# Turning normalised blocks by DMA instead of TensorE, and one more MLP quarter as seven products, in an eight-core decoder step

## What is computed

```python
# layer 0: token mixers A (causal pooling) and B (HGRN2 recurrence, 6 heads)
h = rmsnorm(x, norm_mix[0])
mixed = even_layer(h, ...)            # in-projection, pooling, HGRN2, out-projection
x = x + mixed
x = x + square(relu(rmsnorm(x, norm_mlp[0]) @ ff_w1[0])) @ ff_w2[0]     # d_ff = 4096
# layer 1: short gated convolution
x = x + odd_layer(rmsnorm(x, norm_mix[1]), ...)
x = x + square(relu(rmsnorm(x, norm_mlp[1]) @ ff_w1[1])) @ ff_w2[1]
y = rmsnorm(x, norm_final)
# rmsnorm(x, g) = x * rsqrt(mean(x*x) + eps) * g, over the 1024 channels of a token
```

## Time and profile before

| what | value |
|---|---|
| median of 3 runs | 1490.19 us (1487.7 to 1490.36) |
| the profiled execution, slowest core | 1491.38 us |
| its span, first to last instruction | 1489.6 us |
| spans of the eight cores | 1471.7 to 1489.6 us |
| mean granted TensorE clock of the cores | 0.984 to 0.991 |
| busy share of the span | PE 94%, DVE 72%, ACT 57%, POOL 15% |

### The profile page before, as it was taken

One profiled execution on the slowest core, in us unless ns is written; L12 is line 12 of the kernel. 1 busy time (PEld: TensorE's weight loads), 2 busy tenths in 40 slices (PEclk: granted clock), 3 DMA queues, 4 the chain that ended last, 5 costly groups with the idle time before them and its releaser, 6 DMA issues.

```text
span 1489.6 us, 25207 instructions; the slowest of 8 cores (1471.7 to 1489.6 us)
## 1 busy us (share of the span) xinstructions
PE 1407.6 (94%) x9195; PEld 709.8 (48%) x9195; DVE 1074.0 (72%) x1907; ACT 850.7 (57%) x1715; POOL 217.6 (15%) x286
## 2 busy tenths in 40 slices
PE   4888899999999999999999999999999999999996
PEld 2555455645445444454445544445544444544442
DVE  4799788878565768867767655558676577877767
ACT  4777588865334646854657322236646447755655
POOL 2143443433300100000001000000000000000000
PEclk9899899999999999999999999999999999999999
DMA  7854144477950643633743322300426436654632
GB/s 166 179 83 83 50 83 99 95 146 171 171 125 15 101 73 62 106 62 53 113 72 47 61 43 52 71 15 0 73 45 111 80 51 111 154 103 73 111 72 113
DMA packets 61715, 130.19 MB, mean 87 GB/s; under 512 B 6350, under 2 KB 33084, under 8 KB 61580
## 3 DMA queue, kind: packets, MB, share of 16 engines
q0 software_dynamic: 25952, 90.78, 37.1%
q1 hardware_dynamic: 34028, 37.48, 8.3%
q10 hardware_dynamic: 1616, 0.33, 0.1%
HBM read 203.86 MB, written 15.54 MB: 147 GB/s over the span
## 4 chain that ended last, share of the span: by engine, by line
PE 70%; DMA 13%; DVE 10%; ACT 3%; issue 2%; POOL 1%; ACTq 1%; POOLq 0%; DVEq 0%
PE pp L567 44%; PE pp L565 24%; DMA ring<-w2w 7%; DMA ring<-wst 5%; PE pp L577 2%; ACT arena L505 2%; DVE mixT L531 1%; DVE arena L531 1%; DVE x_sb L543 1%; DMA ring<-w1w 1%; DVE x_sb L531 1%; DVE ring L531 1%; DVE arena L543 1%; DVE arena L1724 1%; DVE hT L531 1%
## 5 line engine op out<-in xcount | busy, mean ns | idle before, releaser
L567 PE MATMUL pp<-hT,ring 128*128 128x512 f16 (+1 forms) x2480 | 459.2, 332 | 8.7 <-DMA ring<-wst 6.1
L531 DVE TENSOR_TENSOR x_sb<-x_sb,pp 128x512 f32<-128x512 f32 x488 | 319.1, 684 | 115.3 <-PE pp L565 42.0
L567 PEld LDWEIGHTS pp<-hT,ring 128*128 128x128 f16 x2480 | 202.5, 98 | 229.5 <-issue 22.2
L505 ACT ACTIVATE pp<-pp 128x512 f32<-128x512 f32 x336 | 192.0, 582 | 204.6 <-PE pp L565 152.0
L567 PE MATMUL pp<-ring,mixT 128*128 128x512 f16 x824 | 191.8, 379 | 3.6 <-DVE mixT L531 1.7
L505 ACT ACTIVATE arena<-arena 128x512 f16<-128x512 f16 (+1 forms) x279 | 169.8, 623 | 35.8 <-DVE arena L1724 30.9
L505 ACT ACTIVATE arena<-pp 128x512 f16<-128x512 f32 (+5 forms) x226 | 124.6, 560 | 115.0 <-PE pp L567 77.3
L565 PE MATMUL pp<-ring,arena 128*128 128x512 f16 x488 | 124.9, 379 | 0.0
L567 PEld LDWEIGHTS pp<-ring,mixT 128*128 128x128 f16 x824 | 77.9, 98 | 92.1 <-issue 6.3
L565 PE MATMUL pp<-hT,ring 128*128 128x512 f16 x448 | 112.8, 379 | 8.0 <-ACT pp L505 8.0
L582 POOL DMA_DIRECT2D ring<-w2w x56 | 29.6, 530 | 464.6 <-PE pp L567 137.8
(11 more groups left out here) (184 smaller groups left out, 1966.7 us busy)
## 6 DMA issues: line engine op xcount, KB each, us to landing
ring<-wst POOLq DMA_DIRECT2D x57, 512.0 KB, 9.2
ring<-w1w POOLq DMA_DIRECT2D x56, 512.0 KB, 6.9
ring<-w2w POOLq DMA_DIRECT2D x56, 512.0 KB, 6.9
x_sb<-xp SPq DMA_DIRECT2D x28, 512.0 KB, 7.3
yp<-x_sb SPq DMA_DIRECT2D x16, 512.0 KB, 2.8
x_sb<-st_hgrn SPq DMA_DIRECT2D x24, 256.0 KB, 5.1
nhs<-x_sb SPq DMA_DIRECT2D x24, 256.0 KB, 6.8
ring<-wst POOLq DMA_DIRECT2D x8, 256.0 KB, 8.3
```

What stands on the lines that cost most here:

```text
L505: return e.activation(out=out, in_=in_, func=func, bias=bias, scale=scale)
L531: return Op(eng, lambda e: e.tensor_tensor(out=out, in0=in0, in1=in1, op=op), R, W, occ, occ + 0.08)
L567: ins = e.matmul(o, l, r, start=s, stop=t)
```

## The change

Norm 1 of blocks 8 to 15 and norms 2 and 3 of all blocks no longer use PE and PSUM. DVE multiplies x by rs and by the gain row in `hg` straight into the junk page, SP writes the page to one of two scratch tensors in DRAM (`rows_d`), and SP reads it back with a DMA that turns it on the way into `hT`. The gain row of norms 1 to 4 is loaded into `hg` by a generator of its own, `grow`, each time when the norms before are done; for norm 1 when the HGRN part no longer needs `hg`. Norm 0 and norm 1 of blocks 0 to 7 stay as they were. `CLASSIC` falls from 2 to 1, so X does three quarters of pair 0 instead of two, and the plain part loads four units less. The planner's DMA clock becomes one clock for each issuing engine behind the HGRN part (`P.split`).

```diff
-CLASSIC = 2
+CLASSIC = 1
...
-        self.dma_free = 0.0
+        self.dma_free = {"all": 0.0}
+        self.split = False
...
-        begin = max(self.dma_free, start + op.occ)
-        self.dma_free = begin + nbytes / (DMA_RATE * 1e6)
-        done = self.dma_free + 2.0
+        q = eng if self.split else "all"
+        begin = max(self.dma_free.get(q, 0.0), start + op.occ)
+        self.dma_free[q] = begin + nbytes / (DMA_RATE * 1e6)
+        done = self.dma_free[q] + 2.0
...
+    rows_d = [nc.dram_tensor(f"rows{i}", [128, 1024], F16, kind="Internal").ap() for i in range(2)]
...
+            if turn:
+                fns = [(lambda e, o=o, i=i: e.dma_start_transpose(out=o, in_=i)) for (o, i) in pairs]
...
+        def grow():
+
+            for n in range(1, 5):
+                if n == 1:
+                    yield up(*[("mix", c, t) for c in range(8) for t in range(4)], "scratch", ("mix", 0, 4), ("mix", 1, 4))
+                else:
+                    yield up(*[("h%d" % (n - 1), b) for b in range(16)])
+                yield DMA("sp", misc(), [(hg[:, :], grows_d[n:n + 1, :].partition_broadcast(128))], (), B_hg, 524288)
+                flags.add(("grow", n))
...
+            elif n > 1 or b >= 8:
+                yield up(("grow", n))
+                yield STT(junk, xb, rs, hg[:, :], ALU.mult, ALU.mult, [Bx, Bn, B_hg], Bj)
+                yield DMA("sp", rows_ds[k], [(rows_d[k], junk)], Bj, [B_rows[k]], 262144)
+                jp.give(it)
+                yield DMA("sp", tr_ds[k], [(hT[:, :, b * 128:b * 128 + 128], rows_d[k])], [B_rows[k]], [B_hT[b]], 262144, turn=True)
+                flags.add(done)
+                return
...
             yield up(("S", LASTHEAD, 2))
             late.append(1)
+            P.split = True
...
-            yield DMA("sp", misc(), [(hg[:, :], gfin_d.partition_broadcast(128))], (), B_hg, 524288)
-            flags.add("gfin")
```

More of the change, by code:

```diff
@@ L392, in build @@
     gcols_d = din("gcols", [128, 40])
-    gfin_d = din("gfin", [1, 1024])
+    grows_d = din("grows", [5, 1024])
+    rows_d = [nc.dram_tensor(f"rows{i}", [128, 1024], F16, kind="Internal").ap() for i in range(2)]
     lbl_d = din("lbl", [128, 18])
@@ L579, in TRG, with DMA @@
             return Op("pe", f, R, W, occ, occ + 0.15, multi=True, margin=margin)
-        def DMA(q, dsem, pairs, R, W, nbytes):
-            fns = [(lambda e, o=o, i=i: e.dma_start(out=o, in_=i)) for (o, i) in pairs]
+        def DMA(q, dsem, pairs, R, W, nbytes, turn=False):
+            if turn:
+                fns = [(lambda e, o=o, i=i: e.dma_start_transpose(out=o, in_=i)) for (o, i) in pairs]
+            else:
+                fns = [(lambda e, o=o, i=i: e.dma_start(out=o, in_=i)) for (o, i) in pairs]
             occ = (0.55 if q == "pool" else 0.06) * len(pairs)
@@ L728, in build @@
         B_hg = [B_S, B_mask, B_wblk]
+        B_rows = [Buf("rows0"), Buf("rows1")]
+        rows_ds = [new_dsem(f"ds_rows{i}") for i in range(2)]
+        tr_ds = [new_dsem(f"ds_tr{i}") for i in range(2)]
+        def grow():
+            for n in range(1, 5):
+                if n == 1:
+                    yield up(*[("mix", c, t) for c in range(8) for t in range(4)], "scratch", ("mix", 0, 4), ("mix", 1, 4))
+                else:
+                    yield up(*[("h%d" % (n - 1), b) for b in range(16)])
+                yield DMA("sp", misc(), [(hg[:, :], grows_d[n:n + 1, :].partition_broadcast(128))], (), B_hg, 524288)
+                flags.add(("grow", n))
         junks0 = Pool([((i, None), [B_mix[i // 2][2 * (i % 2)], B_mix[i // 2][2 * (i % 2) + 1]]) for i in range(4)])
@@ L748, in norm @@
             if n == 4:
-                yield up("gfin")
+                yield up(("grow", 4))
                 yield STT(xb, xb, rs, hg[:, :], ALU.mult, ALU.mult, [Bx, Bn, B_hg], [Bx])
@@ L2067, in build @@
         S.spawn(main(), 300)
+        S.spawn(grow(), 0)
         S.spawn(conv_sample(), 290)
@@ L2179 @@
     w2w = np.stack([_blocks_w2(ff_w2[l]) for l in range(2)])
-    shared = dict(wst=wst, w1w=w1w, w2w=w2w, gcols=gcols, gfin=norm_final.reshape(1, 1024), lbl=lbl, gainf=gainf, pscalef=pscalef,
+    shared = dict(wst=wst, w1w=w1w, w2w=w2w, gcols=gcols, grows=norms, lbl=lbl, gainf=gainf, pscalef=pscalef,
                   poolw=pool_w[0], convwf=convwf, c_identb=identb, c_identh=identh, c_identf=identf, c_maskT=maskT,
```

## The result

The changed kernel takes 1534.78 us (median; 1531.89 to 1542.58), the kernel before 1490.28 beside it: a ratio of 1.031, interval 1.027 to 1.035. I had forecast 1474 and a range up to 1497. All times and ratios here leave disturbed runs out, and each ratio is against the kernel before on the same chip.

What follows compares the result with a forecast made beforehand. TensorE (PE), busy 94% of the span, was taken to bound the kernel. Terms -17.8 (transposes), -4.6 (quarter), +5 (filler) and +0.7 (transfers) sum to -16.7 us, giving 1474 us, range 1460 to 1497.

Steps and rivals of the forecast that it cites:

- the price of the transfers: Stalls of PE behind the norms' DMA writes and turned reads: +0.7 us in all, at the convolution's start.
- PE's work: Transposes of 40 norm blocks leave PE, 0.445 us each, on the path: -17.8 us.
- The quarter: One more quarter of the first pair's MLP with seven products: -4.6 us, between -6.9 and -1.7.
- Rival D: Turning was not on the path outside the two out-projections: -10.7 instead of -17.8, hence 1481; no chance apart from the forecast's 0.62.
- The filler: PE's remaining work during the last HGRN and sample heads about suffices without the moved quarter: +5 us, bounds 0 and 17.
- Rival A: Filler runs out before the second out-projection: 17 us idle between 400 and 430.7, hence 1486; chance 0.14.
- The transfers' landing: Each block's write lands in w = 2.8 us, its turned read in r = 6.8; w + r between 5.6 and 16.0.
- rivals B: Turned read takes twice a plain one, r = 10.2: convolution stalls 14.3 us, second MLP 6, hence 1493; chance 0.10.
- Rival C: Late norms, r = 15.3: stalls of 34.7 and 26.4 us at convolution and second MLP, hence 1534; chance 0.14.
- Who waits for the transfers: Stalls were priced by when PE needs hT; SP's in-order waits were named, ACT and DVE counted 0.
- Wanted only 150 us later: Norm 1's eight blocks are wanted only for pair 1, so gain-row load and transfers are hidden; without cover 41 us.
- The two stalls that I did price: PE waiting for hT: convolution's start +0.7 us (bounds 0 and 26), second MLP's start none (18 at the upper bound).

Runs made afterwards that it cites:

- e5: Changed kernel without the two transfers: VectorE writes the scaled block straight into hT, not turned; 1473.2 us, ratio 0.988.
- e1: Kernel before with only the quarter moved (CLASSIC = 1), norms still turned by TensorE; 1491.3 us, ratio 0.9997.
- e11: Changed kernel with pair 1's first combination of hidden inputs gated in the planner until pair 0's last quarter has begun; 1528.6 us, ratio 1.0268.
- e6: Changed kernel with only norm 1, only norm 2 or only norm 3 turned by DMA, the other two by TensorE; 1504.6, 1514.9 and 1500.0 us.
- e3: Changed kernel with each turned read replaced by a plain read in 256-byte pieces, same order on each engine; 1518.0 us, ratio 1.0199.
- e4: Changed kernel with each turned read moving only the first of a block's eight 128 x 128 tiles; 1508.8 us, ratio 1.0115.
- e9: Changed kernel with only blocks 0 to 11 of norm 3 turned by DMA, all others by TensorE; 1482.9 us, ratio 0.9948.

## Why the prediction was wrong, point by point

The step that failed is the price of the transfers. The sum has +0.7 us for it; e5 shows 61.6. It failed in two ways: one landing time for every write and every read, where the runs show two, and the count of who waits for them.

- **PE's work: right.** -17.8 us for 40 turnings: 1302.9 - 1322.4 = -19.5. The quarter -4.6: 1322.4 - 1327.7 = -5.3. Rival D falls with it. (The bound of -1.7 for double the overhead is a slip, 48.3 + 4.5 - 55.2 = -2.4; nothing hangs on it.)
- **The filler: right on balance.** I had weighed +5 against -4.6; e1 moved the time by nothing that can be told. X opened at 446.24 with a stall of 10.4 us ahead of it, so near 436, where I had 437. Rival A falls. X then lasted 388.8 us instead of 371: 14.4 of the 17.8 us between are the two stalls inside it on weight loads, 5.0 and 9.4.
- **The transfers' landing: mis-sized as one number.** I took w = 2.8 and r = 6.8 for all of them. In the median they are 2.2 and 4.2, so rivals B (from r = 10.2) and C (from w + r = 12.6) seem out. But each is two numbers: w 2.1 and r 3.7 with no weight load beside them, 7.0 and 8.4 with one, and a tenth of those reads above 15.9. Beside loads w + r is 15.4, above the 12.6 from which C decides. I had named the weights in flight for the convolution, and not asked at which hand-over weights are in flight: at all of them. The trace of before had this to read: of the transfers whose landing it gives, the state outputs that lent me r = 6.8 took 8.7 us beside a weight load (32 of them) and 2.3 without (16), and the y outputs that lent me w took 4.5 (48) and 2.7 (80).
- **Who waits for the transfers: counted for readers of hT alone.** The weight loads became late (681.80 and, in e11, 462.01), and so did ACT, which waits for the junk page: 41 us in 12 waits. SP waits for its own writes and reads, the sign that I had named for B and C, and what it issues next is late. These waits overlap, so they don't add up to the 61.6 us. The waits of the changed kernel, SP's from the view of its own queue:

```profile
ACT arena L509 <- DMA rows<-arena: 41.1, 12, 10.6
...
DVE hT L534 <- DMA hT<-rows: 22.2, 3, 11.0
...
SPq L2112 <- DMA rows<-arena: 85.0, 30, 16.6
...
SPq L2112 <- DMA hT<-rows: 32.9, 8, 13.0
```

- **"Wanted only 150 us later": wrong.** That step called norm 1 and the blocks 8 to 15 of norm 3 hidden because PE wants them late. But DVE wants them early: pair 1's first combination stands 5.6 us behind pair 0's, and the trace of before had it to read, with both rows in DVE's timeline:

```profile
484.44 1.23 DVE L531 TENSOR_TENSOR hT<-hT 128x2048 f16<-128x2048 f16 x1 [0.67 <-PE pp L567]
490.08 1.22 DVE L531 TENSOR_TENSOR hT<-hT 128x2048 f16<-128x2048 f16 x1
```

  The gate of e11 shows that this alone was not the loss. The claim of cover was still wrong, and the 41 us that I priced for norm 1 without cover is about three times the 13 of e6.
- **The two stalls that I did price**: the convolution's start +0.7, the second MLP's start 0. Measured 6.4 (and 1.8 behind it) and 9.2. The first came from ACT at its junk page, not from PE waiting for hT at the fifth unit.
- **The clock: not in the sum.** 14 us more are lost at 1.2 GHz, beside 53 us of idle time. Each pause was paid for again by the slow matmuls behind it.
- **Rival C** gave 1534 us and the time is 1534.8, but that the numbers meet is luck: it had every read at 15.3 us and two stalls of 35 and 26. The changed kernel has five stalls of 5 to 10.4 us on its slowest core, from a minority of late transfers, and the clock behind them. What C named for itself, SP in order and weights in flight in the same stretch, is what the trace shows.
- **The Trainium skill's two sentences.** The Trainium skill, "Advanced Engine Details and Errata" (X-Bar Transpose (TRN2)), says that turned transfers are as fast as plain ones. The median landings agree: 3.7 us turned and 3.4 plain for the same pieces with no load beside them, 8.4 and 8.3 with one. The turned kernel is still 17 us slower than e3; its slowest tenth beside loads is later (above 15.9 us against 12.7) and each issue holds SP longer (1.25 us against 0.52), and no run shows which of these makes the 17 us. The Trainium skill, "VectorE: DVE Perf Modes" (The three transpose paths), gives 1309 ns for one 128x128 tile on the crossbar. My estimate from it, 10.5 us for eight tiles one after another, doesn't come out: where nothing stood beside them eight tiles landed in 3.7 us, and one tile in 2.3 (e4).

## What to carry to other kernels

Price a transfer that replaces work on the bounding engine by what else is on the DMA engines at that moment, in both directions, and by what stands behind it in the issuing engine's order: e9 gains 0.5% with twelve turned reads in a stage that loads no weights, and the same read in the other 28 places too makes the kernel 3% slower than before. "Wanted late" has to be read from the streams of all engines that run in order, not from the last consumer. And where removing one stall moves the time little, look for the next transfer to land.

## What the runs showed of the hardware that I had not expected

- A turned read holds SP for 1.25 us at its issue (median; 1.23 to 5.2) where the write of the same block takes 0.34, as the group of SP's instructions on these rows shows (min/median/max, first and last start):

```profile
L589 SPq DMA_DIRECT2D rows<-arena x40: 332/337/1410, 394.1 to 1100.8; - x40
L587 SPq DMA_TRANSPOSE hT<-rows x40: 1231/1250/5205, 396.4 to 1106.6; - x40
```

  In e3 the plain read of the same 256 KB holds SP for 0.52 us. The next writes stand in order behind it.
- A read of an eighth of the bytes takes 2.3 us against 3.7 alone, but 5.8 against 8.4 beside weight loads: most of what a load beside it adds doesn't depend on the size of the read.
- In the profiled execution of the kernel before, of each pair of neighbouring cores (0 and 1, 2 and 3, and so on) one is 11 to 17 us longer than the other (spans 1488.4 and 1471.7, 1484.2 and 1472.8, 1478.7 and 1489.6, 1477.1 and 1487.9), though all do the same work (1326.1 to 1330.3 us at full clock). In 73 other executions of it the difference is 2.9 to 18.2 us, 10 in the median, and either core can be the longer; between neighbours of different pairs the median is 6. The metric takes the longer one. The cause was not looked for.
